# Gate rows moved among the first branch's tiles, second norm folded into diagonal products, a third high slot, and the last down projection and final norm by token tile

## What is computed

```
h   = rmsnorm(x, g1) * (1 + scale1) + shift1
P   = h @ W_in                       # columns of three mixers and three gates
mix = (sum_b sigmoid(gate_b) * (y_b @ W_b)) @ W_out      # b: Hyena, GLA, S5
x   = x + gt1 * mix                  # gt1, gt2: 1024 numbers each, silu(c) @ W_mod + b_mod
h2  = rmsnorm(x, g2) * (1 + scale2) + shift2
x   = x + gt2 * ((silu(h2 @ Wa) * (h2 @ Wb)) @ Wffn_out)     # 2816 hidden columns
out = rmsnorm(x, g_final)
```

## Time and profile before

| | us |
|---|---|
| median of 3 runs | 1621.14 |
| lowest, highest | 1618.27, 1622.38 |
| span of the profiled execution, first to last instruction | 1617.0 |
| TensorE busy in it | 1315.1 (81%) |
| VectorE, ScalarE, GpSimd busy in it | 641.9, 375.6, 356.7 |
| mean granted TensorE clock | 0.865 |

### The profile page before, as it was taken

How to read it: one execution, slowest core, us unless ns; L and a number is a source line. 1 busy time by engine, 2 the same in 40 slices (tenths; PEclk the granted TensorE clock), 3 DMA queues, 4 the chain that set the end, 5 groups by cost and what they waited for, 6 DMA issues and landing times.

```text
span 1617.0 us, 14321 instructions
## 1 busy us (share of the span) xinstructions
PE 1315.1 (81%) x5713; PEld 966.6 (60%) x5713; DVE 641.9 (40%) x999; ACT 375.6 (23%) x462; POOL 356.7 (22%) x149
## 2 busy tenths in 40 slices
PE   6399948797578778776767788499996999999994
PEld 2398735574355556555233344276895888888883
DVE  0502523426676767771455634823334000220022
ACT  2411303031222322213222031001133221122212
POOL 2212400202120211112111001021313555455541
PEclk9699956678787778877789898799997999999998
DMA  9111461103110221214100110132542332333221
GB/s 340 57 53 58 131 100 52 53 26 102 42 33 7 72 46 33 72 33 115 44 13 27 33 39 0 39 131 91 182 147 62 104 86 91 98 105 103 75 71 52
DMA packets 135523, 122.01 MB, mean 75 GB/s; under 512 B 12831, under 2 KB 124666, under 8 KB 135456
## 3 DMA queue, kind: packets, MB, share of 16 engines
q1 hardware_dynamic: 115936, 99.81, 20.4%
q10 hardware_dynamic: 15632, 10.50, 3.0%
q0 software_dynamic: 3888, 10.78, 2.2%
HBM read 114.25 MB, written 4.72 MB: 74 GB/s over the span
## 4 chain that ended last, share of the span: by engine, by line
PE 53%; DVE 19%; issue 3%; ACT 3%; ACTq 1%; POOL 1%; DMA 0%; DVEq 0%; POOLq 0%
PE psum L622 45%; DVE buf L1963 2%; DVE buf L1962 2%; DVE buf L1801 1%; PE psum L817 1%; PE psum L835 1%; DVE buf L1803 1%; PE psum L826 1%; DVE buf L1929 1%; PE psum L773 1%; ACTq L1334 1%; PE psum L926 1%; PE psum L769 1%; DVE buf L1959 1%; DVE hT_hi L2030 1%
## 5 line engine op out<-in xcount | busy, mean ns | idle before, releaser
L1091 POOL TENSOR_TENSOR ring_lo<-buf,ring_hi 128x2048 fp32r<-128x2048 f32 (+1 forms) x65 | 294.0, 4524 | 1020.0 <-ACT ring_hi L1225 1020.0
L622 PE MATMUL psum<-buf,buf 128*128 128x512 f32 (+2 forms) x864 | 314.2, 522 | 90.5 <-DVEq L1489 24.5
L622 PE MATMUL psum<-hT_hi,ring_hi 128*128 128x512 f32 x744 | 311.8, 419 | 17.2 <-DVE hT_lo L2031 15.4
L622 PE MATMUL psum<-hT_lo,ring_hi 128*128 128x512 f32 x744 | 298.0, 401 | 0.0
L622 PE MATMUL psum<-hT_hi,ring_lo 128*128 128x512 f32 x744 | 296.8, 399 | 0.0
L622 PEld LDWEIGHTS psum<-buf,buf 128*128 128x128 f32 (+1 forms) x864 | 146.7, 173 | 244.4 <-issue 126.8
L1225 ACT ACTIVATE ring_hi<-buf 128x2048 fp32r<-128x2048 f32 (+1 forms) x65 | 121.9, 1875 | 323.4 <-PE psum L622 246.7
L622 PEld LDWEIGHTS psum<-hT_hi,ring_hi 128*128 128x128 f32 x744 | 145.8, 196 | 57.8 <-DVE hT_lo L2031 15.6
L622 PEld LDWEIGHTS psum<-hT_lo,ring_hi 128*128 128x128 f32 x744 | 145.5, 196 | 35.0 <-issue 5.4
L622 PEld LDWEIGHTS psum<-hT_hi,ring_lo 128*128 128x128 f32 x744 | 144.9, 195 | 31.5
L2040 DVE TENSOR_TENSOR buf<-psum,buf 128x512 f32<-128x512 f32 x22 | 15.2, 692 | 220.8 <-PE psum L622 220.8
(11 more groups left out here) (316 smaller groups left out, 1796.0 us busy)
## 6 DMA issues: line engine op xcount, KB each, us to landing
buf<-in_w_in SPq DMA_DIRECT2D x26, 1024.0 KB, 5.3
buf<-in_w_mod SPq DMA_DIRECT2D x24, 1024.0 KB, 5.3
buf<-in_w_ffn_in SPq DMA_DIRECT2D x44, 512.0 KB, 5.1
buf<-in_w_ffn_out SPq DMA_DIRECT2D x8, 1024.0 KB, 5.1
buf<-in_w_out SPq DMA_DIRECT2D x4, 1024.0 KB, 5.2
buf<-in_w_ffn_out SPq DMA_DIRECT2D x4, 768.0 KB, 4.4
buf<-in_x ACTq DMA_DIRECT2D x1, 2048.0 KB, 11.8
buf<-in_w_br_gla SPq DMA_DIRECT2D x4, 512.0 KB, 3.5
```

The source lines that it names most:

```text
L622: ins = nc.tensor.matmul(o, a, b, start=start and n == 0, stop=stop and n == len(pairs) - 1)
L1091: nc.gpsimd.tensor_tensor(ring_lo[:, s * SLOT:s * SLOT + size], ring[:, s * SLOT:s * SLOT + size], ring_hi[:, h:h + size].bitcast(fp32), S ...
```

## The change

The eight row steps are put among the first branch's tiles, one behind each branch product, and their loads into `plan` at the same places. The order of loads there becomes gate, branch, row, row, four times, and then W0 to W3. A third high slot lies over the Hyena branch's output and is used from W2 on, free once the last branch product is done. The squares of the second norm are taken on ScalarE by quarters of 256 columns as each output block is added; the scaling of the tiles is left out, and instead VectorE makes, for each token tile, a diagonal matrix of the reciprocals, with which TensorE multiplies the unscaled x in place of the transposition. TensorE waits for h2 slice by slice in the first feed-forward product. In the down projection the token tile becomes the outer loop within a block and the wait covers the block's hidden tiles at once. The final norm's squares are taken by halves on ScalarE as the last blocks are added, each tile's scaling is done in VectorE's queue behind the next tile's addition, in two halves, and SP stores each half tile (256 KB).

```diff
+        ring_hi3 = over("ring_hi3", hy_at, SLOT)
         STEPS, plan, place, cum, split_order = [], [], {}, [0] * RS, []
+        hi_slot, hi_before = [], []
+
+        def take_hi():
+
+            m = len(hi_slot)
+            if wide[0] is not None and m == wide[0] + 2:
+                k = 2
+            elif wide[0] is not None and m > wide[0] + 2:
+                k = hi_slot[m - 3]
+            else:
+                k = m % 2
+            before = [i for i in range(m) if hi_slot[i] == k]
+            hi_slot.append(k)
+            hi_before.append(before[-1] if before else None)
+            return k
+
+        hi_at = {0: ring_hi[:, 0:SLOT], 1: ring_hi[:, SLOT:2 * SLOT], 2: ring_hi3}
+        wide = [None]
...
-            h = (m % HS) * SLOT
+            hi = hi_at[take_hi()] if split else None
...
         beside = list(merge_steps(0))
+        rest = [8, 9, 10, 11, 20, 21, 22, 23]
         while late or beside:
             one_beside()
-        step("mT_split")
-        for i in (8, 9, 10, 11):
-            want(f"mod{i}", block(w_mod, 256 * i), split=False)
-            step("gt", i)
+            if len(beside) % 2 == 0 and rest:
+                i = rest.pop(0)
+                want(f"mod{i}", block(w_mod, 256 * i), split=False)
+                step("gt", i)
+        step("A2")
+        wide[0] = len(split_order)
         for i in range(4):
             want(f"wo{i}", block(I["w_out"][0], 256 * i))
             step("wo", i)
-        step("norm2")
-        for i in (20, 21, 22, 23):
-            want(f"mod{i}", block(w_mod, 256 * i), split=False)
-            step("gt", i)
-        step("A2")
         step("h2T")
...
+        third_from = last_use["br03"] + 1
         for m, name in enumerate(split_order):
             at = first_use[split_order[m - 1]] if m else first_use[name] - 1
             p = place[name][5]
             at = max(at, first_use[plan[p - 2][0]])
-            if m >= HS:
-                at = max(at, last_use[split_order[m - HS]] + 1)
+            if hi_before[m] is not None:
+                at = max(at, last_use[split_order[hi_before[m]]] + 1)
+            else:
+                at = max(at, third_from if hi_slot[m] == 2 else 0)
...
             def h2_T():
-                pe.wait_ge(S("xn2"), 4)
-                for k in range(KD):
+                first = [open_job(f"x2T{k}") for k in range(4)]
+                for t in range(4):
+                    pe.wait_ge(S("diag"), t + 1)
+                    for k in range(4):
+                        ins = nc.tensor.matmul(first[k][:, t * P:(t + 1) * P], xr[:, t, k * P:(k + 1) * P],
+                                               diag[:, t, :], start=True, stop=True)
+                        if t == 3:
+                            close(ins, f"x2T{k}")
+                for k in range(4, KD):
                     name = f"x2T{k}"
                     o = open_job(name)
                     for t in range(4):
-                        ins = nc.tensor.transpose(o[:, t * P:(t + 1) * P], xn2[:, t, k * P:(k + 1) * P], ident)
+                        ins = nc.tensor.matmul(o[:, t * P:(t + 1) * P], xr[:, t, k * P:(k + 1) * P], diag[:, t, :],
+                                               start=True, stop=True)
                     close(ins, name)
-                pe.wait_ge(S("h_split"), 3 * KD)
 
             def ffn(j):
                 views = halves(f"ffn{j}")
                 for nm, (wh, wl) in zip(("fa", "fb"), views):
                     name = f"{nm}{j}"
                     o = open_job(name)
-                    close(product3(o, ((wh[:, k, :], wl[:, k, :], hT_hi[:, k, :], hT_lo[:, k, :])
-                                       for k in range(KD))), name)
+                    for k in range(KD):
+                        if name == "fa0":
+                            pe.wait_ge(S("h_split"), 2 * KD + k + 1)
+                        ins = product3(o, [(wh[:, k, :], wl[:, k, :], hT_hi[:, k, :], hT_lo[:, k, :])],
+                                       start=k == 0, stop=k == KD - 1)
+                    close(ins, name)
                 last_job[f"ffn{j}"] = f"fb{j}"
...
-                for i in range(n):
-                    k = k0 + i
-                    pe.wait_ge(S("act_lo"), hf * NFH + k + 1)
-                    for t in range(4):
-                        c = slice(t * P, (t + 1) * P)
+                pe.wait_ge(S("act_lo"), hf * NFH + k0 + n)
+                for t in range(4):
+                    c = slice(t * P, (t + 1) * P)
+                    for i in range(n):
+                        k = k0 + i
                         ins = product3(acc[0][t], [(act_hi[:, k, c], act_lo[:, k, c], wh[:, i, :], wl[:, i, :])],
                                        start=(k == 0), stop=(k == NFH - 1))
-                        if k == NFH - 1:
-                            close(ins, f"d{hf}{q}{t}")
+                    if k == NFH - 1:
+                        close(ins, f"d{hf}{q}{t}")
...
+            for t in range(4):
+                for h in range(2):
+                    c = slice(512 * h, 512 * h + 512)
+                    sp.wait_ge(S("out"), 2 * t + h + 1)
+                    sp.dma_start(out[0, t * P:(t + 1) * P, c], xr[:, t, c]).then_inc(S("stored"), 16)
+            sp.wait_ge(S("stored"), 128)
...
                 act.wait_ge(w_full[s], c)
-                if m >= HS:
-                    released(act, split_order[m - HS])
-                A(ring_hi[:, h:h + size], ring[:, s * SLOT:s * SLOT + size], ACT.Copy).then_inc(S("w_hi"), 1)
+                if hi_before[m] is not None:
+                    released(act, split_order[hi_before[m]])
+                elif hi_slot[m] == 2:
+                    full(act, f"b0{KD - 1}")
+                A(hi_at[hi_slot[m]][:, 0:size], ring[:, s * SLOT:s * SLOT + size], ACT.Copy).then_inc(S("w_hi"), 1)
...
-            def norm2():
-                full(act, "wo33")
+            def x2_sq(i, t):
+                act.wait_ge(S("x2"), 4 * i + t + 1)
+                if 4 * i + t:
+                    act.wait_ge(S("ss2"), 4 * i + t)
+                c = slice(256 * i, 256 * i + 256)
+                A(junk[:, c], xr[:, t, c], ACT.Square, accum_out=sq2[:, t, i:i + 1]).then_inc(S("ss2"), 1)
+
+            def wo(i):
                 for t in range(4):
...
+                    x2_sq(i, t)
+                    if i == 3 and t:
+                        x2_rt(t - 1)
+                if i == 3:
+                    x2_rt(3)
+
+            def x2_rt(t):
+                act.wait_ge(S("ms2"), t + 1)
+                A(rs2[:, t:t + 1], ss2[:, t:t + 1], ACT.Sqrt, scale=1.0 / D, bias=epsc).then_inc(S("sd2"), 1)
...
+            def down_ev(hf, q):
+                if hf == 0:
+                    return
+                c = slice(512 * q, 512 * q + 512)
                 for t in range(4):
...
+                    act.wait_ge(S("x3"), 4 * q + t + 1)
+                    if 4 * q + t:
+                        act.wait_ge(S("ssf"), 4 * q + t)
+                    A(junkf[:, c], xr[:, t, c], ACT.Square, accum_out=sqf[:, t, q:q + 1]).then_inc(S("ssf"), 1)
+                    if q and t:
+                        final(t - 1)
+                if q:
+                    final(3)
+
+            def final(t):
+                act.wait_ge(S("msf"), t + 1)
+                A(rsf[:, t:t + 1], ssf[:, t:t + 1], ACT.Sqrt, scale=1.0 / D, bias=epsc).then_inc(S("sdf"), 1)
...
-                    link(V.tensor_tensor(xr[:, t, c], xr[:, t, c], xtmp[:, 0:256], ADD))
-                    if i == 3:
-                        signal("x2")
...
+                    V.tensor_tensor(xr[:, t, c], xr[:, t, c], xtmp[:, 0:256], ADD).then_inc(S("x2"), 1)
+                    dve.wait_ge(S("x2"), 4 * i + t + 1)
+                    if i == 3 and t:
+                        norm2(t - 1)
+                if i == 3:
+                    norm2(3)
+
+            def norm2(t):
+                dve.wait_ge(S("ss2"), 12 + t + 1)
+                V.reduce_sum(ss2[:, t:t + 1], sq2[:, t, :], AX).then_inc(S("ms2"), 1)
+                dve.wait_ge(S("sd2"), t + 1)
+                link(V.reciprocal(rs2[:, t:t + 1], rs2[:, t:t + 1]))
+                V.tensor_scalar(diag[:, t, :], ident, rs2[:, t:t + 1], None, MUL).then_inc(S("diag"), 1)
...
-                    link(V.tensor_tensor(xr[:, t, c], xr[:, t, c], xtmp, ADD))
-                    if (hf, q) == (1, 1):
-                        signal("x3")
...
+                    ins = V.tensor_tensor(xr[:, t, c], xr[:, t, c], xtmp, ADD)
+                    if hf:
+                        ins.then_inc(S("x3"), 1)
+                        dve.wait_ge(S("x3"), 4 * q + t + 1)
+                    else:
+                        link(ins)
+                    if (hf, q) == (1, 1) and t:
+                        final(t - 1)
+                if (hf, q) == (1, 1):
+                    final(3)
+
+            def final(t):
+                dve.wait_ge(S("ssf"), 4 + t + 1)
```

(46 more changed lines are left out.)

31 lines of the change are left out of this document (8 added, 23 removed).

## The result

The changed kernel is slower: 1642.05 us median of four runs (1641.92 to 1645.1) against 1620.44 for the kernel before in the same job, a ratio of 1.0138 (95% interval 1.0124 to 1.0152). The forecast was 1650, range 1631 to 1662; it started from a median of 1621.14. The profiled execution has a span of 1640.1 us against 1617.0, 23.1 more.

What follows compares the result with a forecast made beforehand. TensorE was taken as the bound, with only 37.8 us of waits winnable and moved rows opening new holes. Terms 16.2 + 9.6 + 8.4 - 4.0 - 1.0 = +29.2 us on 1621.1 gave 1650 us, range 1631 to 1662.

Steps and rivals of the forecast that it cites:

- Holes at G1 to G3: First branch's tiles: TensorE waits 5.4 us at each of three gate weights, chain 12.3 less cover 6.9; +16.2 us.
- The hole at W0: Ahead of the output projection: last tile's sum, shut out by GpSimd's subtractions, starts W0's product 11.1 us late; +9.6 us.
- The clock: Behind the four new TensorE holes: products restart at the half clock, 2.1 us each; +8.4 us (0 to +12).
- The second norm: Last output product to end of fa0: quarter squares, diagonal products and slice-by-slice start, one collision gone; -4.0 us.
- The third slot does nothing for the rest: Feed-forward part: no gain from the third high slot, since TensorE was already busy 365.05 of 365.1 us.
- The tail: Down projection's last slot and final norm: VectorE ends 0.5 us sooner, SP's half-tile store saves some 0.5; -1.0 us.
- (a): Rival on the moved rows: weights come in time, no holes, only the savings count; 1614.6 us, chance 0.10.
- (b): Rival: holes are there, but the clock holds and the last tile's sum is in time; 1635.8 us, chance 0.15.
- (c): Rival: VectorE holds up the splits, or the norm's chain collides twice; +6 to +12, about 1660 us, chance 0.08.

Runs made afterwards that it cites:

- e1: The changed kernel with all eight rows behind the eight first-branch tiles; 1615.15 us, ratio 0.9956 to the kernel before.
- e2: The changed kernel with both rows of a pair of tiles behind the pair's second branch product, same load order; 1622.74 us, ratio 1.0019 to the kernel before.
- e3: The changed kernel with the last tile's merge ahead of the last row's addition and W0's split behind the last sigmoid; 1636.63 us, ratio 1.0098.
- e8: e1 with only two high slots instead of three; 1609.68 us, ratio 0.9942 to the kernel before.
- e10: The same kernel as e9 but with the third high slot; 1601.3 us, ratio 0.9876 to the kernel before.
- e9: e1 plus later second feed-forward subtraction, early root tables, W0's load ahead of rows 22 and 23, two high slots; 1599.2 us, ratio 0.9865.
- e4: The kernel before with its four whole-tile stores issued by SP instead of GpSimd; 1615.40 us, ratio 0.9970.
- e5: e1 with GpSimd's subtraction of the second feed-forward block waiting until VectorE has written all eight h2 slices; 1607.29 us, ratio 0.9924.
- e6: e1 with the down projection's loops of the kernel before, hidden tile outside and token tile inside; 1617.36 us, ratio 0.9982.

## Why the prediction was right, and which sizes were off

**Holes at G1 to G3** (+16.2): 14.3. The mechanism is shown from three sides: e1 takes the holes away, e2 shrinks them by the cover added, and the change's own timeline has the chain. The chain was 11.6 us and not 12.3, mostly since these loads landed in 5.0 us.

**The hole at W0** (+9.6): 9.5. The path was the one forecast, add in between, cast shut out a second time; e3 removed 6 us by order alone.

**The clock** (+8.4): 6.6 left over in the tiles (6.1 by the time at 0.50) and 2.2 in the output projection, 8.8. The step that no row of before could decide, whether a hole of about 5 us is enough, was decided by the four windows at 0.50. The size of 2.1 each was an average that fitted: behind the three holes it was 1.7, 1.4 and 3.0. That the 1.5 us hole of before cost nothing isn't in the rows named for it; the trace bears it out, with 1.00 from 1152.6 to 1198.0. The Trainium skill's description ("TensorE: Matmul & The Clock Gate", section "HAM oscillation — how this bites in real kernels") of a loop that waits for weights in every turn and starts every turn slow agrees with the trace, three turns of three.

**The second norm** (-4.0): -6.0. Collision and slice-by-slice start came as forecast (one instruction of 4.88 us). To the end of fa0 I had 5.8 + 14.0 + 1.2 = 21.0 us, and it took 21.2: 5.2 to the last diagonal matrix, 14.2 to the last slice, 1.7 to the end of fa0. The miss is mostly the last term, 1.7 for the half clock in fb0. The clock was at 0.50 from 1264.5 to 1267.9, but fa0 ended at 1267.0, so most of its cost was already inside the 21.2; about 0.5 us fell behind fa0, into the feed-forward section. Another 0.4 is in the section before, 27.1 us for my 26.7. The share of the third slot in it was wrong: e8 shows that the slot moved no split there. What moved the first feed-forward split into the projection was the plan, in which the block two before it is now an output block and no longer a row.

**"The third slot does nothing for the rest"**: wrong. It costs 1.8 us in the feed-forward part (359.0 in e10 against 357.1 in e9), though nothing waits for it.

**The tail** (-1.0): -7.3, the largest miss. VectorE's part was -1.6 where I had -0.5. The store was the mis-sized term: 0.5 was put on it, and it gave 5.7, of which e4 puts 5.1 on the issuing queue. I had priced the issue and the landing of one store, and these gained the 0.5 us; I had put nothing on what lies behind the landing, where GpSimd's DRAIN took 4.6 of the 8.2 us. The row that would have told it was the span's end, 1617.0, held against 1609.17 + 2.9. The Trainium skill ("DMA: Bandwidth & Descriptors", section "Latency and other measured facts") puts the first byte at about 1 us from GpSimd and 0.6 us from the others, from which I had estimated 0.4 us. The traces agree as far as the landing goes: the last store landed 2.9 us after its issue before and 2.6 in e4. But the DRAIN, and not this, decides here.

The misses towards too slow are 2.0 on the holes, 2.0 in the norm and 6.3 in the tail. Against them stand the third slot's 1.8, 0.6 more in the feed-forward section, the clock's 0.4 and 1.5 us of start in which nothing was changed (over the runs here that start ends anywhere from 1048.6 to 1051.9). That makes the difference of 6 us between the +29.2 forecast and the +23.1 of the spans (the medians differ by 21.6). The time came out inside the range because the losses, 34.2 us forecast, came as 32.6, by the mechanisms named; the savings, forecast as 5.0, were 13.3. Of the rivals, (a) fell with the second wait in the table, (b) with the clock and the last tile, (c) is outside the interval.

## What to carry to other kernels

A load that waits for its slot to come free has a chain from release to ready, and TensorE's work between the release and the need must cover it; whoever inserts blocks into a ring of loads shortens the lead of all others, so count the cover again for each of them, here 6.9 us against 11.6. In these runs a hole of 2.3 us or more also cost the clock behind it, and an instruction queued behind a waiting one on another engine can turn a 5 us hole into 11. Where two engines shut each other out, let the one with slack wait for the other, as e5 does; and read the end of the span against the last landing, since the queue that ends last may be worth more than the arithmetic ahead of it: give the last store to an engine whose DRAIN is short, here SP.

## What the runs showed of the hardware that I had not expected

- GpSimd's queue ended 4.3 to 4.6 us behind its own last work in every kernel here (its closing DRAIN; 4.3 us behind the last subtraction in the eleven with the store on SP, 4.6 us behind the last landing before). It costs time only where GpSimd is the last engine: with the store in its queue the span ended 8.2 us behind VectorE's last instruction, with the store in SP's 3.1, for the same 512 KB tiles. What the DRAIN does in that time isn't shown.
- Feed-forward tiles whose rounded weights lie in the third slot run 0.25 us longer (11.13 us against 10.88), with no wait in the trace; the next tile has 0.03 more. Two kernels that differ in this alone (e9 and e10) differ by 1.8 us in that part. Whether it is the slot's address or something else about it stays open.
- Single holes of TensorE of 1.5 and 1.6 us left the granted clock at 1.00, five of five (before, e4 and e2). Those of 2.3 and 2.4 us were followed by the 0.50 level within 0.8 us, five of five (e1, e5 to e8), and so were those of 3.8 to 11 us. Two holes of 0.8 and 0.9 us, 2 us apart, at the second norm were followed by 0.50 in e1, e6 and e8, and left 1.00 in the changed kernel, e2, e3 and e5.
- A VectorE operation that is waiting when GpSimd's subtraction ends can get in ahead of the next subtraction, even if that is ready: the add ended at 1192.8, and only then did the second begin to shut out the cast. The second subtraction, recorded from 1192.2, took 4.94 us where the first took 4.51; in e2, where an add was under way at the same point, it was 4.94 again.
